# The decay matrices of a two-layer scan: from masked TensorE sums to rows spread by DMA

## The reference, cut to what matters

```
acs     = cumsum(adt)                           # over the 128 positions of a chunk
decay   = exp(acs[q] - acs[k]) where k <= q, else 0
y_diag  = ((C[q] . B[k]) * decay[q, k]) @ xdt[k]
y       = y_diag + (contribution of the state that the chunk before left)
```

## Time and profile before

| | us |
|---|---|
| median of 3 runs | 2420.59 (2420.19 to 2424.4) |
| the profiled execution: its time | 2423.08 |
| the profiled execution: its span | 2421.3 |
| PE busy | 2084.1 (86%) |
| DVE busy | 1390.3 (57%) |
| POOL busy | 984.7 (41%) |
| ACT busy | 978.0 (40%) |
| mean granted clock of TensorE | 0.94 |

### The profile page before, as it was taken

One profiled execution on the slowest core, in us unless ns is written; L12 is line 12 of the kernel. 1 busy time (PEld: TensorE's weight loads), 2 busy tenths in 40 slices (PEclk: granted clock), 3 DMA queues, 4 the chain that ended last, 5 costly groups with the idle time before them and its releaser, 6 DMA issues.

```text
span 2421.3 us, 27269 instructions
## 1 busy us (share of the span) xinstructions
PE 2084.1 (86%) x9974; PEld 1536.1 (63%) x9974; DVE 1390.3 (57%) x2695; ACT 978.0 (40%) x1742; POOL 984.7 (41%) x562
## 2 busy tenths in 40 slices
PE   6897798749777887778899899989989989998998
PEld 1585566743333333333698677789978977877997
DVE  2785674547666676665256524257743663334776
ACT  1430334322121212221445656345554565544554
POOL 1161236535444444443576536710027753582000
PEclk9899799879998999989999999989999999998999
DMA  8141465369999999999544323445545532353653
GB/s 326 43 132 43 139 209 187 122 265 421 421 422 421 421 421 421 421 421 419 164 162 152 114 70 120 159 147 184 188 147 162 173 114 77 106 174 122 192 183 105
DMA packets 106245, 526.00 MB, mean 217 GB/s; under 512 B 11904, under 2 KB 11904, under 8 KB 72576
## 3 DMA queue, kind: packets, MB, share of 16 engines
q1 hardware_dynamic: 66960, 244.78, 30.9%
q0 software_dynamic: 38720, 275.96, 27.7%
q10 hardware_dynamic: 432, 3.53, 0.3%
HBM read 523.17 MB, written 1.05 MB: 217 GB/s over the span
## 4 chain that ended last, share of the span: by engine, by line
PE 59%; DMA 22%; DVE 8%; ACT 6%; issue 3%; POOL 1%; another core or an unknown queue 1%; SPq 0%; DVEq 0%; ACTq 0%; POOLq 0%
PE psum L785 58%; DMA pair_rows<-in_peer_uv,arena 9%; DMA arena<-in_peer_uv,arena 6%; DMA wring<-in_peer_uv,arena 4%; ACT w_hi L1252 1%; POOL w_lo L2364 1%; DVE arena L1615 1%; ACT arena L1263 1%; PE psum L831 1%; DMA wring<-in_w_ada 1%; ACT arena L1456 1%; ACT a_hi L1259 1%; DVE dve_junk L1615 1%; ACT arena L1268 0%
## 5 line engine op out<-in xcount | busy, mean ns | idle before, releaser
L2364 POOL TENSOR_TENSOR w_lo<-wring,w_hi 128x1024 fp32r<-128x1024 f32 x282 | 692.6, 2467 | 769.7 <-ACT w_hi L1252 730.1
L1252 ACT ACTIVATE w_hi<-wring 128x1024 fp32r<-128x1024 f32 (+1 forms) x414 | 433.8, 1053 | 415.5 <-PE psum L785 360.8
L785 PE MATMUL psum<-w_hi,a_hi 128*128 128x512 f32 (+1 forms) x1056 | 417.4, 395 | 21.4 <-POOL w_lo L2364 12.2
L785 PE MATMUL psum<-arena 128*128 128x512 f32 (+7 forms) x1142 | 333.9, 449 | 95.4 <-ACT arena L1404 53.7
L785 PE MATMUL psum<-w_lo,a_hi 128*128 128x512 f32 (+1 forms) x1056 | 411.3, 389 | 0.0
L785 PE MATMUL psum<-w_hi,a_lo 128*128 128x512 f32 (+1 forms) x1056 | 410.5, 389 | 0.0
L785 PE MATMUL psum<-a_hi,w_hi 128*128 128x256 f32 x1312 | 377.7, 288 | 11.0 <-POOL w_lo L2364 3.9
L785 PE MATMUL psum<-a_lo,w_hi 128*128 128x256 f32 x1312 | 376.5, 287 | 0.0
L785 PE MATMUL psum<-a_hi,w_lo 128*128 128x256 f32 x1312 | 376.1, 287 | 0.0
L785 PEld LDWEIGHTS psum<-arena 128*128 128x128 f32 (+2 forms) x1142 | 182.7, 197 | 231.9 <-issue 167.2
L785 PE MATMUL psum<-pair_rows,arena 128*128 128x512 f32 x512 | 257.2, 656 | 60.2 <-ACT arena L1404 60.2
(11 more groups left out here) (224 smaller groups left out, 2359.7 us busy)
## 6 DMA issues: line engine op xcount, KB each, us to landing
wring<-in_w_up SPq DMA_DIRECT2D x88, 512.0 KB, 3.7
wring<-in_w_xbc SPq DMA_DIRECT2D x48, 512.0 KB, 3.5
wring<-in_w_dn SPq DMA_DIRECT2D x44, 512.0 KB, 3.5
wring<-in_w_adaT SPq DMA_DIRECT2D x32, 512.0 KB, 4.1
wring<-in_w_qkv SPq DMA_DIRECT2D x32, 512.0 KB, 4.2
wring<-in_w_z SPq DMA_DIRECT2D x32, 512.0 KB, 3.5
wring<-in_w_g SPq DMA_DIRECT2D x32, 512.0 KB, 3.5
wring<-in_w_ps SPq DMA_DIRECT2D x32, 512.0 KB, 3.5
```

The lines of the kernel that those rows point to most:

```text
L785: mm = lambda o, a, b, start, stop: nc.tensor.matmul(o, a, b, start=start, stop=stop, skip_group_check=True)
L1252: a.reaches(A(w_hi[:, n % SPLIT_RING, 0:width], wring[:, c % RING, 0:width], ACT.Copy), hi_ready, n + 1)
L2364: nc.gpsimd.tensor_tensor(w_lo[:, r, 0:width], wring[:, c % RING, 0:width], w_hi[:, r, 0:width].bitcast(F32), ALU.subtract).then_inc(lo_re ...
```

## The change

The cumulative sums that the kernel already has (`acs_s`, position on the partitions, chunk and head on the columns) are transposed once per layer by PE (bank "acsT"), copied out by ACT and stored to a DRAM tensor, `acs_rows`, by a DMA on ACT's queue. In the scan, DMAs from ACT's queue load the 4 rows of half a group from there, spread over all 128 partitions (2 KB to each, 256 KB a DMA), into one half of `dve_junk`. ACT then computes `relu(acs[k] - acs[q])` for each head, 128 x 128, and one `exp(-...)` in place over all 8 heads (128 x 1024). Where k > q this is exp(0) = 1 or less, not 0, so the mask moves into `cb`: DVE copies "cb" out of PSUM with the triangle `upto` as a factor (ACT copied it before). The "seg" banks, the constant `after` and `nacs_s` are gone. The products of the gates start before the scan's own products, each after the first is cut in two by the scan's products for an odd i, and DVE's scratch for "yo" moves from `dve_junk` to `Brow`.

```
-        for i in range(SSD_G * TT):
-            g.extend([(L + "seg", 2 * i), (L + "seg", 2 * i + 1)])
...
+        for i in range(0, SSD_G * TT, 2):
+            if i:
+                g.extend([(L + "y", i - 1), (L + "yo", i - 1)])
+            g.extend([(L + "gate", i), (L + "gate", i + 1), (L + "y", i)])
...
+    def decay_rows(l, i, half):
+
+        first = (32 * (i % TT) + HPG * (i // TT) + 4 * half) * P
+        return acs_rows[l:l + 1, first:first + 4 * P].to_broadcast([P, 4 * P])
...
+            pe.wait_ge(S("acs_ready"), l + 1)
+            transposes(L + "acsT", 0, [acs_s])
             attended(1)
...
+            for i in range(0, SSD_G * TT, 2):
+                columns_of_rows("w2_g", l, [(L + "gate", i), (L + "gate", i + 1)], [0, 0], early=True,
+                                before=(lambda n=i - 1: ssd_out(n)) if i else None)
+                ssd_out(i)
             ssd_out(SSD_G * TT - 1)
...
+            read_out(L + "acsT", 0, acsT, bank(L + "acsT", 0)[0:64, 0:P])
+            a.settle()
+            act.dma_start(acs_rows[l].rearrange("(a b) -> a b", b=P), acsT).then_inc(S("acs_stored"), 16)
             attended_out(1)
...
+            act.wait_ge(S("acs_stored"), 16 * (l + 1))
+            for half in range(2):
+                act.dma_start(dve_junk[:, 512 * half:512 * half + 512], decay_rows(l, 0, half)
+                              ).then_inc(S(f"decay_rows_in{half}"), 16)
...
+                    rows = dve_junk[:, 512 * half:512 * half + 512]
+                    act.wait_ge(S(f"decay_rows_in{half}"), 16 * (8 * l + i + 1))
                     for j in range(4):
...
+                        h = 32 * c + g * HPG + 4 * half + j
+                        a.done(A(Lm[:, i % 2, (4 * half + j) * P:(4 * half + j + 1) * P], rows[:, j * P:(j + 1) * P],
+                                 ACT.Relu, bias=acs_s[:, h:h + 1], scale=-1.0))
+                    a.settle()
+                    if i < SSD_G * TT - 1:
+                        act.dma_start(rows, decay_rows(l, i + 1, half)).then_inc(S(f"decay_rows_in{half}"), 16)
+                a.reaches(A(Lm[:, i % 2, :], Lm[:, i % 2, :], ACT.Exp, scale=-1.0), S("decay_exp"), 8 * l + i + 1)
...
+            for c in range(TT):
+                wait_filled(dve, L + "cb", c)
+                readv(L + "cb", c, T.tensor_tensor(cb[:, 4 * c:4 * c + 4, :],
+                                                   bank(L + "cb", c).rearrange("p (g q) -> p g q", q=P),
+                                                   bc(upto, 1, [P, 4, P]), ALU.mult))
...
-                for half in range(2):
-                    wait_read(dve, L + "seg", 2 * i + half)
...
+                dve.wait_ge(S("decay_exp"), 8 * l + i + 1)
```

More of the change, by code:

```diff
@@ L80, in shape_constants @@
     c["ones"] = np.ones((P, P))
-    c["after"] = np.where(l >= k, 0.0, NEG)
     c["causal"] = np.concatenate([np.zeros((P, P)), np.where(l <= k, 0.0, NEG)], 1)
@@ L295, in psum_order @@
         add(L + "p", 2), add(L + "o", 2), add(L + "s", 4, 2)
-        add(L + "z", 2, 4), add(L + "acs"), add(L + "z", 2, 6)
+        add(L + "z", 2, 4), add(L + "acs"), add(L + "z", 2, 6), add(L + "acsT")
         add(L + "p", 4, 2), add(L + "o", 2, 2)
@@ L818, in columns_of_rows @@
                     chunk_used(m)
+            if early:
+                state["turn"] += len(outs)
         def feature_mm(name, l, out_, i):
```

46 lines of the change are left out of this document (8 added, 38 removed).

## The result

| | before | after |
|---|---|---|
| median | 2420.85 (2420.19 to 2424.4, 4 runs) | 2386.01 (2378.35 to 2390.11, 4 runs) |
| the profiled execution: its time | 2423.08 | 2386.79 |
| its span | 2421.3 | 2385.0 |
| mean granted clock of TensorE | 0.94 | 0.936 |

The ratio is 0.984, with a 95% interval from 0.9815 to 0.9865: faster by 34.8 us in the medians and by 36.3 us in the profiled executions. Forecast were 43 us and 2377.5. The runs of after lie further apart than those of before (11.8 us against 4.2).

The account below looks back on a forecast made before the run. PE was taken to bound the scan, busy all 89.2 us. A layer gains 28.0 - 0.9 - (2.1 + 1.3 + 1.3) - 0.8 = 21.6 us; 2420.6 - 43.2 = 2377.5, range 2367 to 2392.

Parts of the forecast that it names:

- "seg" is gone, 28.0 us a layer: Scan on PE: 16 banks of 1.75 us removed, 28.0 us a layer, all on the path; 15.36 us a pair left.
- wrong in kind: Sign of failure: PE's own matmuls in the scan (gates cut in two, "y") take longer than in the earlier trace.
- The store ahead of the probabilities, +0.9 us a layer: Ahead of the scan: ACT's read-out, wait and DMA issue delay the probabilities by 0.9 us, bounds 0.3 and 2.0.
- E: Matmuls behind the scan's new waits run at a slow clock; 5 us if half do, 2382, counted within the forecast's 0.62.
- ACT's pair, 16.65 us: Scan: ACT's work for a pair of i sums to 16.65 us against PE's 15.36, so ACT becomes the bound by 1.3.
- Borders 2.1, 1.3 and 1.3 us, and 0.8 for POOL beside DVE: Scan: PE waits at three borders between pairs, nothing lost at the fourth; 0.8 us added for POOL slowed by DVE.
- Row loads land in 3 to 4 us, hidden: Scan: the 256 KB spread loads land before ACT wants them, with at least 4.6 us of cover; worth 0.
- The tail: Behind the last scan product: it moves with PE and its one wait of 1.78 us stays; change of 0.
- A: Scan: PE stays the bound, ACT fits into 15.36 us; 27.1 us a layer gained, 2366.4 or 2368; chance 0.12.
- B: Scan: row loads come late, ACT waits about 2 us a pair; 6 to 7 us a layer more, 2390 to 2392; chance 0.18.
- C: Scan: row loads set the pace, slower than before; gain eaten from landings of about 11 us, 2440 at 13.6; chance 0.03.
- D: Scan: ACT idles 1.4 us more after each table load; 7 us a layer, 2391.5; chance 0.03.

Follow-up runs that it names:

- the kernel with `zs` in the scan: The change, with DVE's two wide products of the scan output with z cut into eight pieces inside the scan; 2379.58 us.
- the kernel with two buffers: The change, with one 512 KB row load for all 8 heads, two i ahead into one of two buffers, instead of two 256 KB loads; 2377.25 us.
- the clamp on DVE: The kernel with two buffers, with a subtraction and a minimum on DVE in place of ACT's relus; 2397.05 us.
- the kernel with the three edits: The change with 8-head row loads into two buffers, the z product inside the scan, and the store behind the probabilities' copies; 2371.99 us.

## Why the prediction was right, and where it was wrong

The prediction was right: faster, inside the range, for the forecast's own reason. By its steps:

1. **"seg" is gone, 28.0 us a layer.** Right. The even and odd products of the scan take 1.89 and 2.81 us with their overlap, as in the earlier trace rows. A whole pair on PE is a little longer than the 15.36 us of the sum: from 1422.76 to 1438.92, at full clock, it is 16.16 with a wait of 0.56, so 15.6. That is the small form of what the prediction called wrong in kind, 0.24 us a pair; a product of the gates cut in two is 11.46 us in it instead of 11.01, the odd product 2.24 instead of 2.64.

2. **The store ahead of the probabilities, +0.9 us a layer.** The term is about right, and yet "ahead" grew by 2.1 and 2.8 us. From the start of ACT's last copy `w_hi` to its first copy of probabilities it is 1.86 and 2.13 us, where the kernel before has 0.94 and 0.95: the store costs 0.9 and 1.2. The rest is the clock. In layer 0 the matmuls stood some 0.42 us apart from 1368.88 to 1371.40, with a granted clock of 0.61 in that stretch, and PE's chunk took 4.02 us instead of 2.86: 1.2 us more. PE came later itself, and for that reason its wait grew by only 0.37 us (2.07 to 2.44). Layer 1 had such a stretch there before as well. New in it is one behind the wait for the probabilities:

```profile
1979.30 4.94 PE L791 MATMUL psum<-arena 128*128 128x512 f32 x7 [3.12 <-ACT arena L1262]
```

The view ends inside it; the product of eight takes 5.37 us where the kernel before has 3.67 behind a wait of 2.04. I had the clock as E and gave it to the new waits of the scan; here it fell at waits that were there already.

3. **ACT's pair, 16.65 us.** Measured 16.08 in the first pair. The relus are right to 0.01 us, the table too; an issue costs 0.40 us where 0.56 were taken, four of them in a pair, and this is nearly all of the difference. In the second pair ACT also waited 1.12 us for PE's "y" (2.1 us in layer 1, in two waits), so it is not the pacemaker at every moment.

4. **Borders 2.1, 1.3 and 1.3 us, and 0.8 for POOL beside DVE.** The first is 1.69 (1.66 in layer 1). The second is nothing and the third 0.56 (1.27 in layer 1). Two causes: ACT's lag of a pair is 16.08 - 15.6 = 0.5 us and not 1.3, and behind the first wait nine matmuls took 3.64 us (1406.29 to 1409.93) instead of 2.05: 1.6 us of slow clock, in which ACT caught up. So E is not a sum on top of the forecast, as I had it. It took the place of a wait. The kernel with `zs` in the scan shows the same: its layer 0 has such a stretch behind the first wait and two waits, 2.8 us, its layer 1 has none and three waits, 3.8. Waits and slow clock together are 2.25 + 1.6 in layer 0, where 5.5 us of waits were forecast, and the scan is a little shorter than forecast there (gain 23.4 instead of 22.5) and longer in layer 1 (21.1), where two waits had such a stretch behind them (0.79 and 0.83 of the clock).

5. **Row loads land in 3 to 4 us, hidden.** Right: 3.6 us in the median, 3.0 to 5.0. ACT waited for a row twice in layer 0's scan, 1.1 us in all, the longest 0.6; the kernel with two buffers never did.

6. **The tail: it "hangs on the last "y", which moves with PE; its one wait of 1.78 us stays".** This is the step that failed, and it is the largest miss: +3.7 and +3.8 us. I followed PE into the tail and left DVE and POOL out. In the kernel before, ACT copied the first chunks of "pa" late, and POOL stood still for 2.40 us, until 1487.38, in the first part of DVE's product with `zs`. In the change ACT's copies of "pa" come right behind the last sigmoids, POOL has seven chunks in a row, and the product meets POOL at work over its whole length: 8.79 us instead of 6.70. The square root is 2.3 us later behind it (1.3 in layer 1), POOL is later too, and PE waits 3.58 us (3.03 in layer 1) instead of 1.78. That is 1.8 and 1.2 us of the miss. The rest goes for the most part with the clock: in layer 0 seven matmuls right behind that wait stood 0.43 us apart (1481.66 to 1484.64), and the granted clock of the tails is 0.95 and 0.93 instead of 0.96. The wait of 1.78 was in the earlier trace rows, and so was the reason for doubt: step 4 itself had read from the earlier trace rows what POOL loses beside DVE. Moving the product into the scan brought the wait back to 1.77 us and the tails to 93.6 and 95.3.

The mask's move to DVE cost nothing that shows: its two instructions took 1.29 us together. Of the rivals, A and B are wrong (PE waits; ACT waits little for rows), C and D too: a table load is 1.28 us and the next instruction follows at once (1404.60 and 1405.89), so the rule of the Trainium skill (ScalarE: Activation LUTs, section "What ACT_TABLE_LOAD costs") that gives D has its drain of 1.38 us no more in these rows than in the earlier trace rows.

Two sums of the prediction have slips that change nothing: 2420.6 - 43.2 is 2377.4, and rival C says that the fourth border has some 5 us of cover, while its sums 21.4 and 31 take some 9.6. With 5 the gain would be eaten from a landing of 10.1 us on, and the loads landed in 3.6.

In one sum: scan -44.5 (forecast -45.0), ahead +4.9 (+1.8), tail +7.5 (0), scatter elsewhere -4.2 (0). Without that scatter in its favour the profiled execution would have been at 2391, just inside the range: that the time lies as far inside as it does is in part luck.

## What to carry to other kernels

Removing work from the engine that is the bound gives time only if something else fills the place while its new input is made: look for independent work in the same stage and put it there first. When an engine runs ahead of its old schedule, check every pair of engines behind it that now works at the same moment, and not only the waits of the engine that is the bound. Here the engine that had become the pacemaker was relieved by fewer and larger issues, and not by giving its arithmetic to an engine that collides with a busy one.

## What the runs showed of the hardware that I had not expected

**DVE and POOL stop each other for a whole instruction.** A DVE multiplication over 128x512 takes 0.69 us, over 128x1024 1.23, over 128x2048 2.29; a chunk on POOL 2.40. The two products with `zs` took 8.79 us, 4.2 more than 2 x 2.29, and POOL's seven chunks 21.22, 4.4 more than 7 x 2.40; in the kernel before it was 2.1 more, once. The excess comes in portions of about 2.1 us, near the length of one instruction of the other engine: a minimum of 0.69 us takes 2.74 beside POOL. This looks like one engine waiting for the other's instruction, and not like two engines at half speed each. The Trainium skill (SBUF — State Buffer, section "Who interferes with whom") says so: a VectorE instruction with two inputs in SBUF contends with a GpSimd instruction that reads SBUF, one in a mode that uses two ports contends with GpSimd too, and the one that comes second is blocked for the whole instruction of the other. The rows agree. They also show that it can decide where work belongs: with the clamp on DVE the scans are 9.1 and 10.4 us longer than with the relus on ACT, of which the collisions are a part.

**A DMA issue on ACT is short, but not what stands around it.** The issue of a row spread over 128 partitions is 0.33 us, the same for 128, 256 and 512 KB; the gap from the last relu to the next instruction is 0.40 us. At the store of 64x128 the issue is 0.50 and 0.46 us and the gap 0.66 and 0.92. So a load of 8 rows instead of twice 4 is 0.5 us less for each i.

**The slow clock moves time about.** In the change, stretches at 1.2 GHz came behind waits of 1.3 to 3.6 us; in the kernel before none came behind the wait of 2.52 us in layer 0 and the two of 1.78. In the two executions of the change most fell at the same places, but one behind the 1.27 us wait of layer 1 fell in the first alone. One in the scan cost 1.6 us. How much of the change's scatter of 11.8 us that is, no run shows; the kernel with the three edits, with fewer and shorter waits, had a scatter of 2.7 us in its five runs.
